# Both up projections as seven quarter products in every pair but the first, weight sums on GpSimd, taps and gates later

## The reference, cut to what matters

```
u = x @ w_up                       # 1024 -> 2 * 2816
u = causal depthwise convolution of width 3 over tokens, per channel, + conv_b
gate, val = split(u)
out = (silu(gate) * val) @ w_down  # 2816 -> 1024
```

## Time and profile before

| | |
|---|---|
| median of three runs | 1454.0 us |
| the profiled execution | 1446.48 us |
| its span, first to last instruction | 1444.7 us |
| TensorE busy | 98% of the span |
| VectorE busy | 63% |
| ScalarE busy | 23% |
| GpSimd busy | 2% |
| mean granted TensorE clock | 0.994 |

### The profile page before, as it was taken

How to read it: one execution, slowest core, us unless ns; L and a number is a source line. 1 busy time by engine, 2 the same in 40 slices (tenths; PEclk the granted TensorE clock), 3 DMA queues, 4 the chain that set the end, 5 groups by cost and what they waited for, 6 DMA issues and landing times.

```text
span 1444.7 us, 30444 instructions
## 1 busy us (share of the span) xinstructions
PE 1410.2 (98%) x12960; PEld 1288.4 (89%) x12960; DVE 911.2 (63%) x1836; ACT 326.7 (23%) x656; POOL 26.6 (2%) x32
## 2 busy tenths in 40 slices
PE   9999999999999999998899999999999999999997
PEld 8899888999999977778787989999997779999997
DVE  3288433358865473568544887887684447878875
ACT  2134103250000131420121222220103642222211
POOL 0140000000001000000000000000000000000000
PEclk9999999999999999999999999999998999999999
DMA  9435344355444413320000444445543114445451
GB/s 371 161 133 166 113 161 145 117 165 193 166 163 169 158 50 128 131 88 4 5 4 2 147 160 137 169 147 175 187 137 116 52 36 137 158 145 174 149 192 69
DMA packets 56992, 190.73 MB, mean 132 GB/s; under 512 B 9216, under 2 KB 11392, under 8 KB 56608
## 3 DMA queue, kind: packets, MB, share of 16 engines
q1 hardware_dynamic: 50768, 180.93, 37.1%
q10 hardware_dynamic: 6096, 7.91, 1.7%
HBM read 187.77 MB, written 1.05 MB: 131 GB/s over the span
## 4 chain that ended last, share of the span: by engine, by line
PE 93%; DVE 3%; ACT 1%; issue 1%; DMA 0%; ACTq 0%; DVEq 0%; PEldq 0%
PE ps L1886 93%; DVE arena L1674 1%; DMA arena<-in_x_t 0%; DVE arena L1701 0%; PE ps L1171 0%; DVE rs L2371 0%; ACT arena L2319 0%; DVE arena L1702 0%; DVE arena L1625 0%; PE ps L2089 0%; PE ps L1980 0%; DVE arena L1580 0%; DVE arena L865 0%; DVE arena L867 0%; DVE arena L1685 0%
## 5 line engine op out<-in xcount | busy, mean ns | idle before, releaser
L1886 PE MATMUL ps<-arena,ring 128*128 128x128 f32 (+6 forms) x4752 | 819.6, 324 | 3.0 <-PEq L806 0.8
L1886 PEld LDWEIGHTS ps<-arena,ring 128*128 128x128 f32 x4752 | 718.2, 191 | 75.5 <-issue 7.8
L1886 PE MATMUL ps<-arena 64*64 64x64 f32 (+10 forms) x6982 | 572.4, 257 | 13.9 <-issue 6.6
L1886 PEld LDWEIGHTS ps<-arena 128*128 128x128 f32 (+4 forms) x6982 | 514.7, 162 | 44.7 <-issue 23.9
L865 DVE TENSOR_TENSOR arena<-ring 128x512 f32<-128x512 f32 x100 | 69.0, 690 | 119.6 <-PE ps L1886 86.8
L852 ACT COPY arena<-ps 128x128 f32<-128x128 f32 (+2 forms) x72 | 19.2, 266 | 336.9 <-PE ps L1886 336.9
L1651 DVE SCALAR_TENSOR_TENSOR arena<-arena,cols 128x271 f32<-128x271 f32 (+3 forms) x176 | 82.8, 492 | 9.8 <-ACT arena L1312 6.7
L1886 PE MATMUL ps<-arena,consts 128*128 128x260 f32 (+9 forms) x368 | 75.1, 346 | 7.3 <-DVE arena L1829 3.0
L1312 ACT ACTIVATE arena<-arena,cols 128x272 f32<-128x272 f32 (+1 forms) x88 | 48.8, 601 | 122.8 <-DVE arena L1580 68.9
L1886 PEld LDWEIGHTS ps<-arena,consts 128*128 128x128 f32 (+3 forms) x368 | 54.3, 182 | 21.9 <-issue 3.5
L867 DVE TENSOR_TENSOR arena<-arena,ring 128x512 f32<-128x512 f32 x100 | 69.6, 696 | 3.5
(11 more groups left out here) (279 smaller groups left out, 894.8 us busy)
## 6 DMA issues: line engine op xcount, KB each, us to landing
ring<-in_stream SPq DMA_DIRECT2D x342, 512.0 KB, 3.8
consts<-in_consts ACTq DMA_DIRECT2D x1, 1580.0 KB, 12.9
arena<-in_mem_t ACTq DMA_DIRECT2D x1, 1024.0 KB, 7.3
res<-in_x_t ACTq DMA_DIRECT2D x1, 1024.0 KB, 19.2
out_t<-arena SPq DMA_DIRECT2D x4, 256.0 KB, 2.5
arena<-in_x_t ACTq DMA_DIRECT2D x3, 256.0 KB, 5.0
arena<-in_g ACTq DMA_DIRECT2D x1, 640.0 KB, 5.6
arena<-in_w ACTq DMA_DIRECT2D x2, 256.0 KB, 4.5
```

The source lines that it names most:

```text
L1886: return nc.tensor.matmul(out, lhs, rhs, start=start, stop=stop)
```

## The change

Both up projections do every pair except m = 0 in seven products. The sums for pair 1 are still made by VectorE in the stage before; those of pairs 2 to 21 of each layer are made by GpSimd, at the end of its list, on their own semaphore. VectorE scales pair m, then does the gate of pair m - 2, then the taps of pair m - 1, and ScalarE's silu is one pair later too. The first bank set of the products changes from 0 to 4. The buffers are the same.

```diff
-  ("ffa_up", Seven(FIRST["ffa_up"], T2, [4], (0, 4), WIDE, 1, F2, GB, True, 2), 1),
+  ("ffa_up", Seven(FIRST["ffa_up"], T2, [4], (4, 0), WIDE, 1, F2, GB, True), 1),
   (the same for ffb_up)
+        def sums_by_gpsimd(name, i):
+            return name in ("ffa_up", "ffb_up") and i >= 2
+        def sums_before(name, i):
+            return 4 * ((F2 - 2) * (name == "ffb_up") + i - 2)
 TensorE, ffn:
                 for m in range(F2):
-                    if m % 2:
-                        if m == 3:
+                    if m:
+                        if m == 2:
                             pe.wait_ge(rooted, 10 + i)
                         seven_products(pe, mm, up, only=m)
                         continue
 TensorE, seven_products:
                         if p in (6, 7, 3):
-                            pe.wait_ge(w_summed, done + {6: 2, 7: 3, 3: 4}[p])
+                            nth = {6: 2, 7: 3, 3: 4}[p]
+                            if sums_by_gpsimd(name, i):
+                                pe.wait_ge(ups_summed, sums_before(name, i) + nth)
+                            else:
+                                pe.wait_ge(w_summed, done + nth)
 GpSimd:
+        def up_weight_sums(pool, tt, name):
+            y = SEVEN[name]
+            for i in range(2, F2):
+                b, done = y.block(i), sums_before(name, i)
+                a11, a12, a21, a22 = w_quarters(b)
+                s1, s2, s3, s4 = [WSUM[name][y.group(i, 0) % 2][:, x] for x in range(4)]
+                arrived(pool, b)
+                arrived(pool, b + 1)
+                pool.wait_ge(used, y.block(i - 1 if i >= 3 else 0))
+                tt(s1, a21, a22, ALU.add).then_inc(ups_summed, 1)
+                pool.wait_ge(ups_summed, done + 1)
+                tt(s2, s1, a11, ALU.subtract).then_inc(ups_summed, 1)
+                tt(s3, a11, a21, ALU.subtract).then_inc(ups_summed, 1)
+                pool.wait_ge(ups_summed, done + 2)
+                tt(s4, a12, s2, ALU.subtract).then_inc(ups_summed, 1)
 ScalarE, ffn_scalar:
             for m in range(F2):
-                if m % 2:
+                if m:
                     keep_first_product(act, name + "_up", m)
                 (first taps of pair m, as before)
-                (silu of pair m)
+                if m:
+                    silu(m - 1)
+            silu(F2 - 1)
 VectorE, ffn_vector:
+            count_gpsimd_sums(dve, up)
             for m in range(F2):
-                if m % 2:
-                    quads_scaled(up, m, uu[:, (2 * m) % 4:(2 * m) % 4 + 2, :])
-                    if m + 2 < F2:
-                        weight_sums(dve, tt, up, m + 2, 0)
-                else:
-                    (scaling of a direct pair)
-                if m >= F2 - 2:
-                    weight_sums(dve, tt, down, 0, m - F2 + 2)
-                (taps of pair m, gate of pair m, input sums after every fourth)
+                if m:
+                    quads_scaled(up, m, uu[:, (2 * m) % 4:(2 * m) % 4 + 2, :])
+                else:
+                    (scaling of a direct pair)
+                if m >= 2:
+                    gate(m - 2)
+                if m >= 1:
+                    convolve(m - 1)
+                if m >= F2 - 2:
+                    weight_sums(dve, tt, down, 0, m - F2 + 2)
+            gate(F2 - 2)
+            convolve(F2 - 1)
+            gate(F2 - 1)
```

More of the change, by code:

```diff
@@ L374, in program @@
                               ("sb_o", Seven(FIRST["sb_o"], L2 // 2, [4], (0, 4), SPLIT, 1, 4, GB, True), 1),
-                              ("ffb_up", Seven(FIRST["ffb_up"], L2 // 2, [4], (0, 4), WIDE, 1, F2, GB, True, 2), 1),
+                              ("ffb_up", Seven(FIRST["ffb_up"], L2 // 2, [4], (4, 0), WIDE, 1, F2, GB, True), 1),
                               ("ffb_down", Seven(FIRST["ffb_down"], L2 // 2, [4, 4, 3], (4, 0), SPLIT, 0, 4, 0, True), 6)):
@@ L380, in program @@
             n_sums += sums
+        ups_summed = sem("up_weights_summed")
+        def sums_by_gpsimd(name, i):
+            return name in ("ffa_up", "ffb_up") and i >= 2
+        def sums_before(name, i):
+            return 4 * ((F2 - 2) * (name == "ffb_up") + i - 2)
         def product_at(y, i, p, more=1):
@@ L775, in ffn @@
                             pe.wait_ge(ev[before], GB + 8)
-                        elif m:
-                            pe.wait_ge(ev[up], GB + s - 3)
                         for k in range(KT):
@@ L870, in weight_sums, with count_gpsimd_sums @@
             tt(s4, a12, s2, ALU.subtract).then_inc(w_summed, 1)
+        def count_gpsimd_sums(dve, name):
+            dve.wait_ge(w_summed, 4 * SEVEN[name].group(1, 0) + 4)
+            dve.sem_inc(w_summed, 4 * (F2 - 2))
+        def up_weight_sums(pool, tt, name):
[13 more added lines that the diff above has]
+                tt(s4, a12, s2, ALU.subtract).then_inc(ups_summed, 1)
         def x_sums(link, tt, name, at=slice(None)):
@@ L1304, in ffn_scalar, with silu @@
             m0 = layer * (2 + F2)
+            def silu(m):
+                act.wait_ge(conv_done, layer * 2 * F2 + 2 * m + 1)
+                f(cu[:, (2 * m) % 4, :], cu[:, (2 * m) % 4, :], ACT.Silu).then_inc(ffs, 1)
             for m in range(F2):
-                if m % 2:
+                if m:
                     keep_first_product(act, name + "_up", m)
@@ L1313, in ffn_scalar @@
                       bias=cols[:, bc + s:bc + s + 1]).then_inc(ffc, 1)
-                act.wait_ge(conv_done, layer * 2 * F2 + 2 * m + 1)
-                f(cu[:, (2 * m) % 4, :], cu[:, (2 * m) % 4, :], ACT.Silu).then_inc(ffs, 1)
+                if m:
+                    silu(m - 1)
+            silu(F2 - 1)
         def chunk_scalar(act):
@@ L1634, in ffn_vector, with convolve @@
             up, down = name + "_up", name + "_down"
-            for m in range(F2):
-                if m % 2:
-                    quads_scaled(up, m, uu[:, (2 * m) % 4:(2 * m) % 4 + 2, :])
-                    if m + 2 < F2:
-                        weight_sums(dve, tt, up, m + 2, 0)
-                else:
-                    for s in (2 * m, 2 * m + 1):
-                        dve.wait_ge(used, b + s + 1)
-                        tt(uu[:, s % 4, :], gps(3 + 4 * (s % 2), width), rs[:, 0:width], ALU.mult).then_inc(ev[up], 1)
-                if m >= F2 - 2:
-                    weight_sums(dve, tt, down, 0, m - F2 + 2)
+            count_gpsimd_sums(dve, up)
+            def convolve(m):
                 for s in (2 * m, 2 * m + 1):
@@ L1656, in ffn_vector, with gate @@
                             ins.then_inc(conv_done, 1)
+            def gate(m):
                 dve.wait_ge(conv_done, layer * 2 * F2 + 2 * m + 2)
@@ L1662, in ffn_vector @@
                     x_sums(link, tt, down, slice(m // 4 * 2, (m + 1) // 2))
+            for m in range(F2):
+                if m:
+                    quads_scaled(up, m, uu[:, (2 * m) % 4:(2 * m) % 4 + 2, :])
+                else:
+                    for s in range(2):
+                        dve.wait_ge(used, b + s + 1)
+                        tt(uu[:, s, :], gps(3 + 4 * s, width), rs[:, 0:width], ALU.mult).then_inc(ev[up], 1)
+                if m >= 2:
[7 more added lines that the diff above has]
+            gate(F2 - 1)
         def chunk_vector(dve, link, v, tt, cpv, gate_a, variance, inverse):
@@ L2695, in _ @@
                     pool2.reach(ins, "wa_scaled")
+            up_weight_sums(pool, g.tensor_tensor, "ffa_up")
+            up_weight_sums(pool, g.tensor_tensor, "ffb_up")
 def blocks_of(w):
```

## The result

The changed kernel takes 1516.5 us, the median of four runs (1513.7 to 1521.8), against 1452.6 for the kernel before: ratio 1.0458, 95% interval 1.0428 to 1.0488. It is slower by 64 us. I had forecast slower, 1493, range 1439 to 1520. Its profiled execution took 1513.7 us with a span of 1511.9, 67.2 more than before's. The executions of any one of these kernels spread over 7 to 11 us, so single traces are compared stage by stage, not by their ends.

The account below looks back on a forecast made before the run. TensorE, busy 98% of the span, was taken to bound the kernel. Pairs +7.9 to +17.7 us in ffa and +9.6 to +19.4 in ffb, plus 6 a layer at the ends, middle +39: from 1454.0 to 1493, range 1439 to 1520.

Parts of the forecast that it names:

- The mechanism: Both up projections: GpSimd's sums and VectorE's two-input SBUF operations shut each other out, VectorE paces, 1475 to 1515 us; chance 0.55.
- the open point: VectorE's taps: taken as blocked beside GpSimd sums, some lasting 1.3 us instead of 0.5, though no row showed it.
- TensorE's gain: Both up projections: ten direct pairs a layer become seven products, 16.0 us less TensorE work at most.
- The time of a pair: In ffa's up projection: four pairs at 6.6 us, then fourteen at 7.9 (8.6); in ffb all 0.2 less.
- the two bounds of GpSimd's operation: One GpSimd sum: lasts 1.04 us and shuts VectorE out for 0.84, or lasts 1.27 and shuts it out for 1.07.
- the middle that I took: Whole kernel: +39 us, between +29.5 and +49, as the nearest row didn't settle how long a GpSimd sum lasts.
- TensorE to idle 1 to 2 us in each pair: Sign in both up projections: TensorE idle 1 to 2 us a pair, waiting for VectorE's scaling.
- The end of each stage: After pair 21, VectorE's remaining work delays the down projection's third group: 6 us a layer, bounds 0 and 9.
- the working's own bounds: Whole kernel: pair times and stage ends of both layers together, +29.5 to +49 us.
- TensorE pacing: Rival, both up projections: taps don't share the path, so TensorE goes on pacing; -13 us, 1441; chance 0.25.
- GpSimd pacing: Rival, both up projections: each GpSimd sum waits for one tap, 7.4 us a pair; +25, with ends 1482; chance 0.08.
- all in series: Rival, both up projections: 9.5 and 9.3 us a pair; +42, +44 and 12, 1552 us; chance 0.07.

Follow-up runs that it names:

- the half change: The kernel before, with only the weight sums of pairs 3, 5 ... 21 moved to GpSimd: 1457.1 us, ratio 1.0042.

## Why the prediction was right, and where its sum was not

**The mechanism.** It is the one forecast: GpSimd's sums and VectorE's two-operand SBUF operations exclude each other, VectorE paces, and TensorE waits for the scaling. The tap was the open point, since no row of before showed one beside GpSimd. Taps at a mean of 0.8 us with the sums and at 0.50 without them (the run without sums) settle it. The rule of the Trainium skill's page "SBUF — State Buffer" (Who interferes with whom), that such a VectorE instruction contends with a GpSimd one that reads SBUF and not with one that only writes it, is borne out for the reading side by VectorE's stretched operations and the sums at 1.35 to 1.50 us. For the writing side the trace agrees in the two taps and some thirty multiplies that ran beside a memset, and no more than that.

**TensorE's gain.** Forecast -16.0 us over both stages; the run without sums and without the early start is 0.8% under the kernel before, 12 us by the ratio, where -13 had been worked out with the ends.

**The time of a pair.** Forecast 7.9 to 8.6 us once VectorE paces, 6.6 for the first four. Pair 2 starts at 833.2 and pair 21 ends at 996.8 in the trace after: 163.5 us, 8.2 a pair, of which VectorE waited 8.5 us in all for TensorE. Without these waits VectorE's pace was (163.5 - 8.5) / 20 = 7.75. The sum has 146.1 to 155.9 us for the same stretch (159.9 and 169.7 less the 13.8 of pairs 0 and 1), 7.3 to 7.8 a pair, so it came out at the upper end. Of the two bounds of GpSimd's operation the longer was right: on ring operands it takes 1.26 undisturbed and shuts out for 1.07, and the middle that I took was too low. I had expected TensorE to idle 1 to 2 us in each pair. It was 25 us in the stage, but mostly gathered into a stall of 5 us before every fourth pair, behind VectorE's input sums, and that brought in the next term.

**What the sum left out: the clock.** I priced TensorE's work after a stall at full speed. Pairs 8, 12, 16 and 20 of ffa follow a stall of about 5 us each and take 7.95, 8.64, 9.00 and 9.18 us from start to start instead of 6.49: 8.8 us. In ffb pairs 10, 12, 16 and 20 lose 10.2 the same way against 6.25. That time is not hidden, because VectorE, which was late, has caught up meanwhile and waits for TensorE. With it and the start of the stage (2.7 and 3.0 us, below) the working gives 19.4 to 29.2 in ffa (7.9 to 17.7, and 11.5), and 28 was measured; in ffb 22.8 to 32.6 (9.6 to 19.4, and 13.2), against 35 measured. The missing 2 us of ffb were not traced.

**The start of each stage.** I had GpSimd's first four sums in free time. They lie beside VectorE's weight and input sums for pair 1: 2.4 and 1.5 us of stall, and 1.1 more in ffb for ScalarE. From the first direct pair to pair 1 TensorE takes 11.0 us instead of 8.25 in ffa and 11.2 instead of 8.2 in ffb, 2.7 and 3.0 more. In the run with them later both stalls are gone.

**The end of each stage.** Forecast +6 a layer. In the trace after, the third group of the down projection starts 14.4 us after pair 21 in ffa instead of 12.97, 1.5 us more, and in ffb 1.7. VectorE catches up within the last pairs, since GpSimd has stopped: pair 21 starts without a stall. What is left are 1.2 and 1.4 us of waits for the down projection's weight sums, which the runs without sums have too, so they come from the new order and not from the lateness. I had carried the lateness too far: 12 forecast, 3 measured.

**The sum.** +39 was forecast and +64 measured, 67 between the two traces. From 39 to these 67 the pair's time makes up 11 us, at the upper end of its bounds, which allow 10; the clock and the starts were missing (19 and 6); the ends were 9 too high; 1 is left over. The direction and the mechanism were right, and the size was not: the working's own bounds were +29.5 to +49. That 1516.5 lies within the range, which reached further, up to 1520, owes something to luck, since the ends' excess stood against part of what was missing. Of the rivals, TensorE pacing would have needed the taps to be free; GpSimd pacing is excluded by the list of waits, which has no wait for GpSimd; all in series would have been 1552. The new order as the cause is excluded by the run without sums.

## What to carry to other kernels

Before moving an operation to an idle engine, add up what the two engines share, not what each has to do: a sum that cost VectorE 0.6 us shut it out for 1.07 when GpSimd made it, and one engine doing everything was 36 us quicker than the two together. Where the receiving engine is nearly full, find the share of the work that fits it (three pairs in four here, from two budgets in the profile) instead of all or nothing. Price a new stall of the matmul engine with the slow stretch behind it, and check first what the helper runs beside at the very start of a stage.

## What the runs showed of the hardware that was not expected

- The shared path seems to be held for less than GpSimd's instruction lasts: VectorE's operations were 1.07 longer beside GpSimd's of 1.26 (0.84 beside 1.04 before). Spans of GpSimd in a profile are rough, so the 0.2 us between the two are rough as well.
- A 128x512 fp32 operation with two inputs takes GpSimd 1.04 us in some places (the multiply of a scaling, the add at L2663 of before) and 1.26 in others (the sums of the ring's quarters, the add at L2653), all undisturbed. What tells them apart was not tested.
- GpSimd's memset of 128x512 fp32 takes 0.52 us, and two taps that ran beside one took their usual 0.50 and 0.49.
- After about 5 us without work TensorE's granted clock was at its lower level of 1.2 GHz for one product and part of the next two, which cost 1.5 to 2.7 us per stall in ffa. Shorter stalls differ: after stalls of 2.05, 2.04 and 3.40 us in ffb the next product took its usual time, but after another of 2.05 the pair took 1.8 us longer, and in the half change the clock was down after one of 2.53.
- With 54 us of useless matmuls in place of the stalls the kernel was 18 us faster.
